# Five landing places at the opening, and GpSimd-moved landing slabs with unskewed passes in the first expert stage

## The reference

```python
def first_block(x, c, ...):
    mod = jax.nn.silu(c) @ w_ada[l] + b_ada[l]                 # 1024 x 6144
    sh1, sc1, gt1, sh2, sc2, gt2 = [m[:, None, :] for m in jnp.split(mod, 6, axis=-1)]
    h = rms_norm(x, g_pre_mix[l]) * (1 + sc1) + sh1
    y = hybrid_mixer(h, w_in[l], ...)                          # w_in: 1024 x 2320
    x = x + gt1 * rms_norm(y, g_post_mix[l])
    h = rms_norm(x, g_pre_ffn[l]) * (1 + sc2) + sh2
    y = moe_ffn(h, w_router, b_router, w_mlp1, b_mlp1, w_mlp2, b_mlp2)
    return x + gt2 * rms_norm(y, g_post_ffn[l])
...
    # moe_ffn: 32 experts, the best 4 of each token, softmax over these 4
    u = xb @ w_mlp1[e] + b_mlp1[e]                             # 1024 x 2048
    x_glu, x_lin = jnp.minimum(u[..., ::2], 7.0), jnp.clip(u[..., 1::2], -7.0, 7.0)
    a = x_glu * jax.nn.sigmoid(1.702 * x_glu) * (x_lin + 1)
    return a @ w_mlp2[e] + b_mlp2[e]                           # 1024 x 1024
```

## Time and profile before

| | us |
|---|---|
| median of 3 runs | 2651.13 (2649.66 to 2653.61) |
| the profiled execution | 2654.19 |
| its span, first to last instruction | 2652.4 |
| PE busy | 2120.5 (80%) |
| DVE, ACT, POOL busy | 500.4, 392.1, 87.4 |
| DMA, mean rate over the span | 257 GB/s |

### The profile page before, as it was taken

How to read it: one execution, slowest core, us unless ns; L and a number is a source line. 1 busy time by engine, 2 the same in 40 slices (tenths; PEclk the granted TensorE clock), 3 DMA queues, 4 the chain that set the end, 5 groups by cost and what they waited for, 6 DMA issues and landing times.

```text
span 2652.4 us, 34466 instructions
## 1 busy us (share of the span) xinstructions
PE 2120.5 (80%) x14230; PEld 1185.3 (45%) x14231; DVE 500.4 (19%) x1153; ACT 392.1 (15%) x864; POOL 87.4 (3%) x130
## 2 busy tenths in 40 slices
PE   4976769567767966979779886899969898977785
PEld 3856422112212211322227766689955546453443
DVE  1044421001101100111120375200041302230002
ACT  1142101001101100111111333100001113110011
POOL 4000000000000000000000000000000000000000
PEclk9995779779888987989899995999979999978898
DMA  9460589999999699997952581346424243079964
GB/s 304 121 244 13 208 364 396 426 425 386 384 425 383 284 426 426 373 399 300 384 199 106 197 291 53 127 159 158 136 103 143 104 134 127 32 299 393 391 261 191
DMA packets 170904, 681.33 MB, mean 257 GB/s; under 512 B 15906, under 2 KB 57123, under 8 KB 125520
## 3 DMA queue, kind: packets, MB, share of 16 engines
q1 hardware_dynamic: 149488, 535.79, 52.0%
q0 software_dynamic: 21328, 144.45, 14.1%
q10 hardware_dynamic: 16, 0.02, 0.0%
HBM read 679.17 MB, written 1.06 MB: 256 GB/s over the span
## 4 chain that ended last, share of the span: by engine, by line
PE 61%; DMA 27%; DVE 6%; ACT 3%; issue 2%; SPq 1%; POOLq 0%; DVEq 0%; POOL 0%; ACTq 0%
PE ps L669 29%; DMA scr<-in_w_mlp 20%; PE ps L985 7%; PE ps L1013 6%; DMA MOD<-in_w 5%; PE ps L1284 3%; PE ps L1024 2%; PE ps L746 2%; DMA ring<-in_w_ada 1%; PE ps L704 1%; PE ps L848 1%; PE ps L756 1%; PE ps L956 1%; DVE stat L1749 1%; PE ps L991 1%
## 5 line engine op out<-in xcount | busy, mean ns | idle before, releaser
L985 PE MATMUL ps<-ring,scr 128*32 128x512 f32 x2208 | 289.2, 656 | 65.7 <-DMA ring<-in_w_mlp 63.4
L669 PE MATMUL ps<-ring,HTY 128*128 128x512 f32 (+5 forms) x960 | 331.0, 506 | 3.7 <-ACT HTY L1365 3.7
L669 PE MATMUL ps<-HTY,ring 128*128 128x256 f32 x1136 | 253.1, 386 | 2.4 <-ACT HTY L1365 2.4
L1013 PE MATMUL ps<-scr 128*32 128x512 f32 x736 | 119.9, 782 | 166.9 <-DMA scr<-in_w_mlp 166.9
L669 PEld LDWEIGHTS ps<-ring,HTY 128*128 128x128 f32 x960 | 176.5, 192 | 155.1 <-issue 138.8
L669 PEld LDWEIGHTS ps<-HTY,ring 128*128 128x128 f32 x1136 | 218.2, 193 | 36.1 <-ACT HTY L1365 3.7
L2117 DVE TENSOR_SCALAR scr<-ps 128x256 f32<-128x256 f32 x46 | 19.6, 425 | 822.6 <-PE ps L991 822.5
L985 PEld LDWEIGHTS ps<-ring,scr 128*32 128x32 f32 x2208 | 64.3, 117 | 215.6 <-issue 131.0
L1365 ACT ACTIVATE scr<-ps 128x512 f32<-128x512 f32 (+8 forms) x120 | 59.1, 494 | 527.4 <-PE ps L669 416.5
L1013 PEld LDWEIGHTS ps<-scr 128*32 128x32 f32 x736 | 25.1, 129 | 241.8 <-DMA scr<-in_w_mlp 185.8
L669 PE MATMUL ps<-ring,scr 128*128 128x128 f32 (+1 forms) x1040 | 121.6, 280 | 1.4 <-DVE scr L2221 1.4
(11 more groups left out here) (416 smaller groups left out, 2039.5 us busy)
## 6 DMA issues: line engine op xcount, KB each, us to landing
ring<-in_w_mlp SPq DMA_DIRECT2D x96, 2048.0 KB, 14.3
scr<-in_w_mlp POOLq DMA_DIRECT2D x32, 2048.0 KB, 23.9
MOD<-in_w_mlp SPq DMA_DIRECT2D x32, 2048.0 KB, 19.0
HTY<-in_w_mlp POOLq DMA_DIRECT2D x32, 2048.0 KB, 18.9
ring<-in_w_ada SPq DMA_DIRECT2D x24, 2048.0 KB, 9.1
ring<-in_w SPq DMA_DIRECT2D x48, 1024.0 KB, 10.4
ring<-in_w_in SPq DMA_DIRECT2D x21, 2048.0 KB, 7.8
ring<-in_w_ff SPq DMA_DIRECT2D x16, 2048.0 KB, 8.8
```

Of the source, the lines that this page charges most:

```text
L669: mm = pe.matmul(o, lhs(k), rhs(k), start=begin and k == 0, stop=end and k == nk - 1)
L985: mm = pe.matmul(ps[C1 * c:C1 * (c + 1), 0, :], XG[:, 2 * j + i, :], m1_slabs[j][:, i, BANK * c:BANK * (c + 1)], start=j + i == 0, stop=False)
L1013: mm = pe.matmul(ps[r:r + C1, 1, :], aT[:, i, C1 * c:C1 * (c + 1)], m1_slabs[j][:, 2 * t + i, BANK * half:BANK * (half + 1)], start=j + i ...
```

## The change

1. **Five places at the opening.** The first five slabs get places of their own: three in `ring`, one in `scr`, one in `MOD`. The sixth slab waits until the first is used up, as each slab waits for the one three places before it in the kernel before. The four `ada1a` slabs come in the order 2, 3, 0, 1 (scale first), and PE makes the narrow products of one before it spreads the one before. DVE prepares the gain and multiplies both halves before the shift is there. POOL issues the three constants of `rel`, does its fills, and holds the other 24 and two vectors back until the first `in1` slab has landed.
2. **Two landing slabs in the expert stage.** Slabs 0 and 1 of the coming expert land in `m1_arrivals` (two slabs, `scr` columns 1024 to 9215), and POOL copies each into `ring` when the place is free.
3. **One queue.** SP issues all six slabs in the order 2, 3, 4, 5, then 0 and 1 of the expert after.
4. **Passes not skewed.** `up` of all four slabs, then hidden values, then `down` of the same pass.
5. The routing's work on `PASSED1` is done in halves and its last two large operations are replaced by small ones; `BD` and `QD` share memory with the expert stage's small tiles and are zeroed again behind it; four vectors are loaded after the stage.

```diff
+def place(s):
+
+    return s if s < SLOTS + EARLY else (s - SLOTS - EARLY) % SLOTS
+
...
-                if s >= SLOTS:
-                    sp.wait_ge(product_ready, release[s - SLOTS])
+                if s >= SLOTS + EARLY:
+                    sp.wait_ge(product_ready, release[s - SLOTS - (EARLY if s < 2 * SLOTS + EARLY else 0)])
...
+            for i in first_gains:
+                column_slabs(I["w_ada"][0], wide[i:i + 2], ada_view)
             column_slabs(I["w_in"][0], [0, 512, 1024, 1536, 2048, 2320])
...
                 sp.dma_start(b1row[0:P:32, :], I["b_mlp1"][0][bass.ds(e, 1), :].rearrange("e (c n) -> (e c) n", c=4))\
                     .then_inc(m1_row_landed, 16)
 
+            def next_expert(e, begin):
+
+                through = sp.value_load(work[0:1, bass.ds(e + (THROUGH - 1), 1)], min_val=1, max_val=PASSES)
+                for j in (2, 3):
+                    sp.wait_ge(m1_slab_used[j], through)
+                    expert_slab(e, j)
+                sp.wait_ge(m1["up"], through)
+                expert_row(e)
+                for j in (4, 5):
+                    sp.wait_ge(m1_slab_used[j], through)
+                    expert_slab(e, j)
+                if begin:
+                    for j in range(2):
+                        sp.wait_ge(m1_moved[j], e + 1)
+                        expert_slab(e + 1, j, m1_arrivals[j])
+
+            sp.wait_ge(mix_ready, 1)
+            expert_slab(0, 5)
+            for j in range(2):
+                expert_slab(1, j, m1_arrivals[j])
             sp.wait_ge(product_ready, end["out1"])
-            for j in range(3):
-                expert_slab(0, j)
+            for j in range(2):
+                sp.dma_start(m1_slabs[j], I["w_mlp1"][0][0][2 * P * j:2 * P * (j + 1), :].rearrange("(p k) n -> p k n", p=P)).then_inc(m1_first_landed[j], 16)
+            expert_slab(0, 2)
             sp.wait_ge(h2_ready, NT)
             expert_slab(0, 3)
             expert_row(0)
+            sp.wait_ge(product_ready, end["route1"])
...
-                sp.wait_ge(m1["up"], through)
-                expert_slab(e, 3)
-                expert_row(e)
+            with sp.Fori(1, E1 - 1) as e:
+                next_expert(e, True)
+            next_expert(E1 - 1, False)
...
-                const(tab[0:32, :], I["rel_bias_2"].rearrange("h b -> b h"))
+                const(flip, I["c_flip"], rel_consts_landed)
+                const(onehot, I["c_onehot"], rel_consts_landed)
+                const(tab[0:32, :], I["rel_bias_2"].rearrange("h b -> b h"), rel_consts_landed)
+                for i, (area, value) in enumerate(((tab[32:33, :], 1.0), (ones[:, :], 1.0), (BD[:, :, :, :], 0.0),
+                                                   (QD[:, :, :, :, :], 0.0), (KC[:, :, :], 0.0))):
+                    pool.memset(area, value).then_inc(zeros_ready, 1)
+                    pool.wait_ge(zeros_ready, i + 1)
+                pool.wait_ge(slab_landed[place(first_slab["in1"])], landed[first_slab["in1"]])
...
             pool.wait_ge(m1["counted"], 1)
             with pool.Fori(1, E1) as e:
                 through = pool.value_load(work[0:1, bass.ds(e + (THROUGH - 1), 1)], min_val=1, max_val=PASSES)
-                pool.wait_ge(m1["down_begun"], through)
-                expert_slab(e, 4)
-                pool.wait_ge(m1["down"], through)
-                expert_slab(e, 5)
+                for j in range(2):
+                    pool.wait_ge(m1_landed[j], 16 * e)
+                    pool.wait_ge(m1_slab_used[j], through)
+                    pool.sem_inc(m1_moving, 1)
+                    pool.tensor_copy(m1_slabs[j], m1_arrivals[j]).then_inc(m1_moved[j], 1)
 
...
-            vector(7)
+            for area in (BD, QD):
+                pool.memset(area, 0.0).then_inc(zeros_again, 1)
+            for v in range(4, 8):
+                vector(v)
 
...
-
-            pe.wait_ge(consts_landed, 16 * n_consts)
+            parts = [0] * 4
+            for x in range(5):
+                if x < 4:
+                    mod_parts(first_slab["ada1a"] + x, 0, first_gains[x])
+                    parts[x] = done[0]
+                if x >= 1:
+                    mod_spread(parts[x - 1], ada_halves[(x - 1) % 2])
+
+            pe.wait_ge(rel_consts_landed, 16 * n_rel)
             pe.wait_ge(zeros_ready, 5)
...
+                    if j < 2:
+                        pe.wait_ge(m1_moved[j], e + 1)
+                    else:
+                        if j == 3:
+                            pe.wait_ge(m1_row_landed, 16 * e + 16)
+                        pe.wait_ge(m1_landed[j], 16 * e + 16)
                     for i in range(2):
                         for c in range(STRIPS1):
                             mm = pe.matmul(ps[C1 * c:C1 * (c + 1), 0, :], XG[:, 2 * j + i, :],
                                            m1_slabs[j][:, i, BANK * c:BANK * (c + 1)], start=j + i == 0, stop=False)
-                    if j < 3:
-                        mm.then_inc(m1_slab_used[j], 1)
-                if b == 1:
-                    for c in range(STRIPS1):
-                        mm = pe.matmul(ps[C1 * c:C1 * (c + 1), 0, :], ones[32 * c:32 * c + 1, 0:C1], b1row[32 * c:32 * c + 1, :],
-                                       start=False, stop=True)
-                    mm.then_inc(m1["up"], 1)
+                    mm.then_inc(m1_slab_used[j], 1)
+                for c in range(STRIPS1):
+                    mm = pe.matmul(ps[C1 * c:C1 * (c + 1), 0, :], ones[32 * c:32 * c + 1, 0:C1], b1row[32 * c:32 * c + 1, :],
+                                   start=False, stop=True)
...
-            def expert_pass(n, e, e_before):
+            def expert_pass(n, e):
 
                 pe.wait_ge(m1["gather_read"], n + 1)
-                up(n, 0, e)
-                turn_hidden(n - 1)
+                up(n, e)
+                if isinstance(n, int):
+                    start_sums()
+                else:
+                    scatter(n - 1)
+                back(n)
+                turn_hidden(n)
                 gather(n + 1)
-                down(n - 1, e_before)
+                down(n, e, 4)
                 turn_tokens(n + 1)
-                up(n, 1, e)
-                scatter(n - 1)
-                back(n)
+                down(n, e, 5)
 
             pe.sem_inc(m1["scatter"], 1)
...
-            def first_scale():
-                dve.wait_ge(product_free, end["ada1a"])
-                gain_scale(1)
-
-            rms_modulate(X, 0, 1, h1_ready, first_scale)
+            for a in range(NT):
+                moments(X[:, a, :], a)
+            inverse_roots(NT, 1e-6, square=True)
+            dve.wait_ge(product_free, first["ada1a"] + 5)
+            gain_scale(1)
+            for a in range(NT):
+                step(dve.scalar_tensor_tensor(H[:, a, :], X[:, a, :], rstd[:, a:a + 1], MOD[:, 1, :], ALU.mult, ALU.mult))
+            dve.wait_ge(product_free, end["ada1a"])
+            for a in range(NT):
+                tell(dve.tensor_tensor(H[:, a, :], H[:, a, :], MOD[:, 0, :], ALU.add), h1_ready, a + 1)
```

244 lines of the change are left out of this document (116 added, 128 removed).

## The result

The changed kernel runs in 2603.86 us (median of 4 runs, 2599.32 to 2613.69), the kernel before, beside it on the same chip, in 2650.39 (2648.98 to 2653.61). The ratio is 0.9818, with a 95% interval of 0.9801 to 0.9834: 46.5 us faster. The profiled execution took 2603.54 us with a span of 2601.5; that of before had 2652.4. The spans differ by 50.9 us, more than the medians, because before's profiled execution lies 3 to 4 us above its median. The forecast was 2603.

What follows compares the result with a forecast made beforehand. DMA was taken to bound the opening and the expert stage's waits; 19.4 + 28.1 = 47.5 us off the profiled 2654.2 gives 2606.7, less 3.1 to the median 2603.6, say 2603; range 2583 to 2634.

Steps and rivals of the forecast that it cites:

- What bounds the kernel: Opening and expert stage wait for DMA; the expert stage lies 103 us short of full use at 426 GB/s.
- The opening: Before in1: fourth slab at 33.0 us instead of 49.3, chain 3.1 us shorter; 19.4 us gained, ends 12 and 22.
- The unskewed pass: Expert stage: a pass without waits for data takes 16.3 us instead of 15.72.
- Experts of several passes: Expert stage: losses become 11.5 us (five single), 37.2 (two of three passes), 8.5 (three in a row); 28.1 won with start and end.
- The copies: POOL's copies of the landing slabs in the expert stage: 3.5 us each, 6.9 if reading costs as much as writing.
- Hidden: Expert stage: POOL's copies cost no time, done by about 9 us of a last pass, next up at 16.3.
- last tenths: Last passes: DVE's two hidden-value operations would meet only the last tenths of a 3.5 us copy.
- The rival of copies in DVE's way: Expert stage: copies delay DVE or cost twice as much, cancelling the 28 us; 2631 us, chance 0.18.
- At 6.9 just hidden: Last passes: even copies of 6.9 us, done at 15.6 us, would still be hidden before the next up at 16.3.
- The rival of POOL as the bound: Expert stage: POOL bounds above 14.7 us a copy, gains used up at 15.5; slower than before, chance 0.04.
- One queue: Expert stage: one queue loses no rate against two; up to 1% of 900 us possible, taken as 0, end 8.
- The term of 1.7 us: End of the expert stage: the last expert's two extra passes and last scatter cost 1.7 us more, leaving 1.5 won.

Runs made afterwards that it cites:

- e3: The kernel before with only the 24 constants and two vectors held back until the first in1 slab: 2634.94 us (ratio 0.9938).
- e12: The changed kernel with whole copies, the second copy of an expert held until DVE has finished the hidden values: 2591.9 us (ratio 0.9760).
- e6: The changed kernel with each POOL copy cut into eight pieces of 512 columns: 2587.81 us (ratio 0.9751).
- e7: The changed kernel with the copies made as 8192 two-byte elements, the same bytes: 2710.11 us (ratio 1.0204).
- e8: The changed kernel with slabs 4 and 5 issued by GpSimd on its own queue behind its copies: 2698.59 us (ratio 1.0169).
- e9: e8 with SyncE held until GpSimd has issued slab 5, to restore the changed kernel's order on two queues: 2725.17 us (ratio 1.0259).
- e11: The changed kernel with each POOL copy cut into two pieces of 2048 columns: 2608.34 us (ratio 0.9823).
- e10: e6 with each up-projection product waiting only for the piece it reads: 2603.99 us (ratio 0.9813).
- e4: The kernel before with the opening's changes only, but the constants sent at once behind POOL's fills: 2646.84 us (ratio 0.9978).

## Why the prediction was right, by its own steps

The result, 46.5 us, lies 1 us from the forecast's 47.5. That is partly luck. By the traces the opening brought 4.9 us more than its term and the expert stage 4.3 more, while 0.4 and 5.4 us were given back, which makes the 50.9 between the spans; the medians differ by some 4 us less, since before's profiled execution lies high. And the expert stage's 32.4 us are what is left after a cost that the forecast put at nothing and I had put among the rivals, 12 to 16 us of DVE held up by copies.

- **What bounds the kernel**: right. Both stages give the gain, and the halves alone add up (21.7 + 26.6).
- **The opening**, forecast 19.4: 21.6 at `in1`, 24.3 behind its first products. The fourth slab came at 31.97 (33.0 taken). The chain from there to `in1` shrank by 4.3 (3.1 forecast). What the term lacked is `in1`'s own start: its first 64 products take 14.08 us at a granted clock of 1.00, against 16.79 at 0.84 in the kernel before and 17.02 at 0.82 in e3. Constants or places: the bandwidth was the greater part, 16.5 of 21.7.
- **The unskewed pass**: 16.19 us between gates 844.19, 860.38 and 876.57 (16.3 forecast).
- **Experts of several passes**, from rates in windows against 426 GB/s: the five single ones lose 9.2 us (11.5), the two of three passes 34.7 (37.2), the three in a row 5.3 (8.5). That is 8.0 better than the forecast's sum. (The 98 us that the prediction adds up come from its windows one by one; the values it writes out, 6.4 for each of four and 22.2 for each of two, give 96.)
- **The copies**: 3.60 us (3.5): right. "Hidden": wrong in six passes and at the start. The prediction let them meet DVE by "last tenths"; there they met it by 2.5 us, since the second copy awaits its landing and starts at the gates, not at 1.8 + 3.5 us of the pass. In the four passes where nothing had to be awaited they met by 0.08 us, as it said. By the medians e12 wins 12 us back and e6 16 (15 and 18 by the ratios). The rival of copies in DVE's way was thus true of the mechanism; it fell short of its 28 us, as the copies were of 3.6 us.
- "At 6.9 just hidden": wrong. At 7.01 (e7) the kernel is slower than before, by 56 us. The rival of POOL as the bound put that point at 15.5 us a copy; it had counted the copies' own time and not what DVE waits.
- **One queue**, taken at 0 to 8: as a matter of rate that holds (425 and 426 GB/s). But with landing slabs two queues cost 95 us (e8), and the kernel before already had 20 slabs 5 overtaken: the term of one queue was thought of as rate alone and left out the order of arrival. The Trainium skill's "DMA: Bandwidth & Descriptors" (Issuing engines are not separate DMA queues) fits the rate, and the page's other section, named at e9, would have warned of the overtaking; the prediction had not drawn on it.
- The prediction gave 1382.87 to the earlier trace rows; it is the start of the last `scatter` in before's timeline and stands in no row. The term of 1.7 us that used it was not tested.
- **Behind the stage** 5.4 us went back, from 1267.5 us to 1272.9. No run tested why, and the cause stays open. Kernels with the same instructions there differ as much among themselves: 1271.4 us in e6's trace, 1276.2 in e12's, 1279.4 in e11's. So differences of some us between medians are not all the stage's, and e11's 2608.34 is no loss against 2603.86.

## What to carry to other kernels

A landing place and a copy buy prefetch across a point where a buffer must stay in use; here they are worth 52 us. Before adding copies on GpSimd, look at which of DVE's operations in SBUF can run beside them, and whether somebody waits for that one: cut the copy into pieces shorter than the wait that can be borne (two halves won nothing here), or hold it behind the operation. Keep slabs that are wanted in order on one queue, and hold back small constants until the first slabs are there. e6 beats both kernels (2587.8).

## What the runs showed of the hardware

- A GpSimd copy from SBUF to SBUF moves 4096 four-byte elements a partition in 3.60 us, 0.88 ns each, and 8192 two-byte elements in 7.01: the time goes by elements, not by bytes.
- Beside it the DVE operations with two SBUF inputs, and `TENSOR_SCALAR`, `CAST` and `COPY` from SBUF to SBUF down to two elements, lasted to the running copy's end (2.90 us for 0.42; 3.50 for 0.20; in e8 a `COPY` of 128x2 up to 3.43 for 0.17). Operations that read PSUM (0.42), `TENSOR_REDUCE` (0.22) and `RECIPROCAL` (0.17) ran in their usual time (e6 above; e8 beside a whole copy).
- In the pass shown at e10, PE waited 7.67 us in one piece in e6 and the low clock lay on the products right behind (3.64 us for 16); in e10 it waited in small pieces, and the low clock lay some 14 us later (1.00 from 560 to 570 us, 0.71 from 570 to 581).
- With two queues full, slabs issued later on one landed before a slab issued earlier on the other (31 of 32 slabs 5 in e9, 20 in e8 and in the kernel before); on one queue none of 192 did.
- With small constants among the slabs the DMA engines moved 213 to 231 GB/s (before, e4) though they show as fully busy; without them 386 (e3).
